# The first layer's modulation: half of its vector moved from TensorE to products on GpSimd and row sums on ScalarE

## The reference, cut to what matters

```python
mod = jax.nn.silu(c) @ ada_w[l] + ada_b[l]        # ada_w: (2, 1024, 6144); the same with c_ctx
sh1, sc1, g1, sh2, sc2, g2 = jnp.split(mod, 6, axis=-1)
h = _rms_norm(x, norm1_g) * (1 + sc1) + sh1
proj = h @ w_in                                   # then three head groups on slices of proj
mix = jnp.concatenate([o_a, o_b, o_c], axis=-1) @ w_out
x = x + g1 * mix
h2 = _rms_norm(x, norm2_g) * (1 + sc2) + sh2
x = x + g2 * (jnp.square(jax.nn.relu(h2 @ w_ff1)) @ w_ff2)
```

## Time and profile before

| | us |
|---|---|
| median of 3 runs (lowest, highest) | 1972.09 (1968.6, 1974.33) |
| the profiled execution | 1966.85 |
| its span | 1965.1 |
| TensorE busy in the span | 1847.0 (94%) |
| VectorE busy | 1092.5 (56%) |
| ScalarE busy | 681.3 (35%) |
| GpSimd busy | 468.1 (24%) |

### The profile page before, as it was taken

How to read it: one execution, slowest core, us unless ns; L and a number is a source line. 1 busy time by engine, 2 the same in 40 slices (tenths; PEclk the granted TensorE clock), 3 DMA queues, 4 the chain that set the end, 5 groups by cost and what they waited for, 6 DMA issues and landing times. The chain is left out here.

```text
span 1965.1 us, 32477 instructions
## 1 busy us (share of the span) xinstructions
PE 1847.0 (94%) x13959; PEld 1750.8 (89%) x13959; DVE 1092.5 (56%) x1629; ACT 681.3 (35%) x1045; POOL 468.1 (24%) x334
## 2 busy tenths in 40 slices
PE   5999989887999999999999999988799999999996
PEld 3899967676999999999999997667799999999996
DVE  3687765665645676766655576557564232323332
ACT  2464346422342131312336534652223223131231
POOL 4000010344342140503530001014524204031244
PEclk9999999998999999999999999989899999999998
DMA  8643120101133444444231212010121212221211
GB/s 350 246 173 90 65 71 2 39 2 60 65 140 108 151 147 157 146 146 144 69 138 66 74 69 71 1 39 2 49 76 66 85 65 74 78 86 65 86 44 54
DMA packets 50527, 179.70 MB, mean 91 GB/s; under 512 B 21616, under 2 KB 23408, under 8 KB 34768
## 3 DMA queue, kind: packets, MB, share of 16 engines
q1 hardware_dynamic: 48848, 176.14, 25.7%
q10 hardware_dynamic: 1536, 1.48, 0.2%
HBM read 168.84 MB, written 8.68 MB: 90 GB/s over the span
## 5 line engine op out<-in xcount | busy, mean ns | idle before, releaser
L1491 PE MATMUL PS<-HH,HI 128*128 128x322 f32 (+1 forms) x1792 | 417.4, 314 | 4.7 <-DVE HL L980 4.7
L1491 PE MATMUL PS<-HL,HI 128*128 128x322 f32 (+1 forms) x1792 | 414.3, 312 | 0.0
L1491 PE MATMUL PS<-HH,LO 128*128 128x322 f32 (+1 forms) x1792 | 413.5, 312 | 0.0
L641 ACT CAST HI<-RAW 128x2048 fp32r<-128x2048 f32 x96 | 182.9, 1905 | 469.3 <-PE PS L1491 442.5
L1491 PEld LDWEIGHTS PS<-HH,HI 128*128 128x128 f32 x1792 | 303.1, 190 | 5.2 <-issue 5.1
L1491 PEld LDWEIGHTS PS<-HH,LO 128*128 128x128 f32 x1792 | 305.3, 191 | 0.0
L1491 PEld LDWEIGHTS PS<-HL,HI 128*128 128x128 f32 x1792 | 304.3, 191 | 0.0
L1491 PE MATMUL PS<-FH,HI 128*128 128x320 f32 x1280 | 293.1, 310 | 1.4 <-DVE FLO L1382 1.4
L1491 PE MATMUL PS<-FH,LO 128*128 128x320 f32 x1280 | 291.4, 309 | 0.0
L973 DVE TENSOR_TENSOR LO<-RAW,HI 128x2048 fp32r<-128x2048 f32 x96 | 232.6, 2423 | 99.5 <-ACT HI L641 99.5
L1491 PE MATMUL PS<-FL,HI 128*128 128x320 f32 x1152 | 262.5, 309 | 0.0
(11 more groups left out here) (282 smaller groups left out, 2254.1 us busy)
## 6 DMA issues: line engine op xcount, KB each, us to landing
RAW<-ws SPq DMA_DIRECT2D x96, 1024.0 KB, 4.9
WM<-adt SPq DMA_DIRECT2D x48, 512.0 KB, 3.6
ADA<-ada SPq DMA_DIRECT2D x16, 1024.0 KB, 7.4
WMX<-adt SPq DMA_DIRECT2D x16, 512.0 KB, 3.7
X<-xT SPq DMA_DIRECT2D x1, 2560.0 KB, 15.7
X<-xT SPq DMA_DIRECT2D x2, 1280.0 KB, 5.9
xs<-X SPq DMA_DIRECT2D x1, 2560.0 KB, 7.9
X<-xs SPq DMA_DIRECT2D x2, 1280.0 KB, 5.5
```

What stands on the lines that cost most here:

```text
L641: nc.scalar.copy(HI[g % 2][:, :], RAW[g % 2][:, :]).then_inc(hi_ready, 1)
L1491: last = pe.matmul(bank(2 * u + a)[:, 0:e], w[:, cols], m[:, a, 0:e], start=(k == 0 and f), stop=(k == KT - 1 and e_))
```

## The change

Columns 16 to 31 leave TensorE. For each of the 16 columns GpSimd multiplies a 128x1024 tile of transposed weights (`WMY`, two buffers, loaded by SyncE) with each condition into `PP[0]` and `PP[1]`, and ScalarE sums `PP[g]` along its row with an accumulating Identity, in place, into `MODN`. GpSimd makes a product of column `n` only when ScalarE has summed the same condition's product of column `n - 1`. ScalarE's sums stand in slots 2 to 12, behind `tile_out`, as many columns a slot as `MOD_IN` says. TensorE's pieces and turns, VectorE's copies and the 1 MB loads go. The new loads stand in SyncE's program behind the slot's `WMX` loads and wait for GpSimd's products. VectorE's slot 13 and ScalarE's slot 21 wait for all products, slot 18 for all sums. The weights are laid out a second way on the host (`adt` gets 16 more tiles).

```diff
+        WMY = [place(f"WMY{i}", [P, D], F32, r_t + i * 4096) for i in range(2)]
+        PP = [place(f"PP{g}", [P, D], F32, r_o + g * 4096) for g in range(2)]
@@ SyncE
-                    def ada_load(j):
-                        sp.dma_start(ADA[3 * (j % 2)][:, :, :], t["ada"][0, 8 + j]).then_inc(ada_in[j % 2], 16)
+                    def gate_load(n):
+                        sp.dma_start(WMY[n % 2][:, :], t["adt"][MF + MT + n]).then_inc(gw_in[n % 2], 16)
@@ SyncE, slot s, behind the WMX loads of the slot
-                        if l == 0 and 1 <= s <= 6:
-                            sp.wait_ge(S["ada_mm"], o["ada_mm"] + s)
-                            ada_load(s + 1)
+                        if l == 0 and s in MOD_IN:
+                            first = sum(MOD_IN[x] for x in MOD_IN if x < s)
+                            for n in range(first + 2, min(first + MOD_IN[s] + 2, MF)):
+                                sp.wait_ge(gprod, 2 * n - 2)
+                                gate_load(n)
@@ GpSimd, ahead of the clearing of LW
+                    def gate_products(n):
+                        if n == 0:
+                            pool.wait_ge(silu_c, 2)
+                        pool.wait_ge(gw_in[n % 2], 16 * (n // 2 + 1))
+                        for g in range(2):
+                            if n:
+                                pool.wait_ge(gsum, 2 * n - 1 + g)
+                            nc.gpsimd.tensor_tensor(PP[g][:, :], WMY[n % 2][:, :], CBX[:, g, :], ALU.mult).then_inc(gprod, 1)
+                    if l == 0:
+                        for n in range(MF):
+                            gate_products(n)
@@ ScalarE, slot j
                         if j == Z0 + 1 and l == 0:
-                            act.wait_ge(S["ada_mm"], 8)
+                            act.wait_ge(gprod, 2 * MF)
                         if j >= 1:
                             tile_out(j - 1)
...
+                        first = sum(MOD_IN[x] for x in MOD_IN if x < j)
+                        for n in range(first, first + MOD_IN.get(j, 0) if l == 0 else first):
+                            for g in range(2):
+                                act.wait_ge(gprod, 2 * n + g + 1)
+                                nc.scalar.activation(PP[g][:, :], PP[g][:, :], ACT.Identity,
+                                                     accum_out=MODN[:, 2 * KT + n, g:g + 1]).then_inc(gsum, 1)
                         if 0 <= j - 3 < 12:
                             conv_silu(j - 3)
@@ ScalarE, slot 18
-                            if l == 0:
-                                act.wait_ge(S["ada_tr"], 8)
@@ VectorE
-                        if l == 0 and 2 <= j <= 9:
-                            ada_row(j - 2)
@@ VectorE, slot 13 and slot 18
+                            dve.wait_ge(gprod, 2 * MF)
-                                dve.wait_ge(S["ada_tr"], 8)
+                                dve.wait_ge(gsum, 2 * MF)
                                 dve.wait_ge(modn, MF)
-                                link(ada_bias(2 * KT, 4 * KT, VEC[:, 2 * KT:4 * KT]))
-                                link(row_bias(4 * KT, 6 * KT, VEC))
+                                link(row_bias(2 * KT, 6 * KT, VEC))
@@ TensorE, slot j
-                        if l == 0 and 1 <= j <= 8:
-                            ada(j - 1)
-                        if l == 0 and 2 <= j <= 9:
-                            adt(j - 2)
```

More of the change, by code:

```diff
@@ L124 @@
     xtr=4, xa=16, xb=16, xo=4, xhi=8, xlo=8, f1_re=32, f1_hi=32, f1_sq=32, f1_lo=32,
-    ada_mm=8, ada_ev=8, ada_tr=8, mod_done=1, moda_done=2)
+    mod_done=1, moda_done=2)
 def build(nc, t):
@@ L324, in build @@
         pro_mm, pro_ev, pro_tr, pro_mod = sem("pro_mm"), sem("pro_ev"), sem("pro_tr"), sem("pro_mod")
-        ada_in = [sem("ada_in0"), sem("ada_in1")]
+        gw_in, gprod, gsum = [sem("gw_in0"), sem("gw_in1")], sem("gprod"), sem("gsum")
         y_fg, y_out = sem("y_fg"), sem("y_out")
@@ L418, in _ @@
                     if l == 0:
-                        ada_load(0)
-                        ada_load(1)
+                        gate_load(0)
+                        gate_load(1)
                     for s in range(PT_ - 2):
@@ L1036, in _ @@
                     o, g0 = base(l), l * CHUNKS
[L1038 to L1044, removed]
                     def taps(i):
@@ L1521, in _ @@
                     o, g0, t0 = base(l), l * CHUNKS, l * TILES
[L1523 to L1533, removed]
                     pe.wait_ge(S["h_sl"], 2 * l + 1)
@@ L1977, in lay_out @@
         "ada": c(tiles(a["ada_w"][0:1], AC).reshape(1, 6 * D // AC, P, KT, AC)),
-        "adt": c(np.concatenate([a["ada_w"][0].T.reshape(MT, P, D)[MT - MF:], a["ada_w"][1].T.reshape(MT, P, D)])),
+        "adt": c(np.concatenate([a["ada_w"][0].T.reshape(MT, P, D)[MT - MF:], a["ada_w"][1].T.reshape(MT, P, D),
+                                 a["ada_w"][0].T.reshape(MT, P, D)[MF:2 * MF]])),
         "crow": c(np.stack([a["c"][0], a["c_ctx"]]).reshape(2, D)),
```

## The result

The changed kernel takes 2029.15 us (median of 4 runs, 2027.02 to 2030.88) against 1971.9 us before (median of 4). The ratio is 1.0291 (95% interval 1.0272 to 1.031): 57 us slower. The forecast was 2024 us, the range 2003 to 2046. The two profiled executions, 1966.85 and 2030.88 us, lie 64.0 us apart, 6.8 more than the medians. What follows on slots is read from these two, so its sums are of 64 and not of 57; where the 6.8 lie isn't shown.

The account below looks back on a forecast made before the run. TensorE was taken to set the pace, VectorE close behind. Products' 61.5 us on VectorE less 3.3 of copies and some 6 of cover gave 52: 1965.1 to 2017 us, 2024 against the median, range 2003 to 2046.

Parts of the forecast that it names:

- TensorE's saving is worth nothing: Slots 2 to 12: the 13.8 us that TensorE saves fall into its waits and win nothing.
- The prices: Slots with modulation: a GpSimd product of 128x1024 takes 2.35 us, a ScalarE row sum 1.25 us.
- Exclusion: Slots 2 to 11: GpSimd products and VectorE operations with two SBUF inputs take turns; 2005 to 2043 us, chance 0.76.
- 2.05 us per product, less 6 of cover: Slots 2 to 11: 30 products each add 2.05 us to VectorE, less 3.3 for copies, some 6 cover: 52.
- the walk: VectorE's odd and even slots followed step by step: 17.5 us becomes 29.2, +11.7 per pair, 52 over slots 2-11.
- The lead: TensorE cannot keep its 9.0 us lead over VectorE at slot 12, so tile 13 is late by about 52 us.
- Its signs: In the profile after: GpSimd busy 75 to 110 us, sums up to 3.5, TensorE's eviction waits 40 to 65, clock unchanged.
- The gain arrives: Slots with modulation: products find VectorE idle or are not held, TensorE's 13.8 us come off; 1958 to 1969 us, chance 0.03.
- nothing moves: Slots with modulation: VectorE goes on at its pace as the true second bound; 1966 to 1978 us, chance 0.02.
- GpSimd gives way: VectorE is always served first, GpSimd is late, splits and taps slip; 10 to 28 us, 1982 to 2000, chance 0.07.
- The queues lock together: ScalarE waits for products, VectorE for ScalarE, TensorE for copies; 3 to 6 us more per pair, 2043 to 2060, chance 0.12.

Follow-up runs that it names:

- when everything went: Changed kernel without products, row sums and their loads, TensorE's gate pieces also gone: 1963.9 us, 3.3 under before, ratio 0.9979.
- The same queue with and without reads: Changed kernel with third weight buffer and loads ahead of modulation loads: 2024.44 us, 57.2 over before; with memsets replacing its products: 1973.81 us, 6.4 over.
- the run with early loads: Changed kernel with a third buffer for the product's weights, their loads ahead of the modulation loads in SyncE's queue: 2024.44 us, ratio 1.0291.

## Why the prediction was right

**TensorE's saving is worth nothing.** Right: by the rows it is 13.8 us, and only 3.3 came off the time when everything went. VectorE's near bound was read rightly from its slots.

**The prices.** Right. The products of the changed kernel (min, median, max in ns):

```profile
L543 POOL TENSOR_TENSOR PP<-WMY,CBX x32: 2339/2446/4438, 67.1 to 221.7; 128x1024 f32<-128x1024 f32 x32
L747 ACT ACTIVATE PP<-PP x32: 1039/1057/1066, 70.5 to 229.9; 128x1024 f32<-128x1024 f32 x32
L747 ACT ACTIVATION_READ_ACCUMULATOR PP<-PP x32: 183/186/188, 71.5 to 230.8; 128x1 f32 x32
```

2339 ns where nothing holds them (2.35 said), and 1057 + 186 ns for a sum (1.06 + 0.19).

**Exclusion.** Shown: products alone on the kernel before cost 58.7 us, their cycle with a sum is 3.34 us (3.31 said), and a sum is back at 1221 ns beside memsets. The same queue with and without reads is 57.2 against 6.4, of which the shorter memsets can explain 23 at most. That only VectorE operations with two SBUF inputs are held was wrong: in the groups above a TENSOR_SCALAR of 40 columns with one tile as input took 2428 ns, 0.18 before. In the changed kernel such small operations lost some 5.5 us.

**2.05 us per product, less 6 of cover.** The term was a little large by itself: 1.83 at full width with 32 in a row, 1.7 with 8, and at half width 0.73 for 0.97. The sum, 52, came out at 62.3 in VectorE's slots: the products hold VectorE directly for only 37.6 us, 1.25 each, but its waits for ScalarE add 26.5, of which the walk had counted the split's in the even slots, and slot 8's as nearly nothing. Two terms of the walk were clearly too small. Slot 5 was taken as any odd slot (4 us), but its exponentials stand behind the sums too: VectorE waits 8.8 us there, and the slot grew by 8.5, from 9.6 to 18.1. And slot 8 grew by 11.3, from 13.1 to 24.4, where the walk's even slot had 7.7 and 1 or 2 on top. By pairs, from slots 2 and 3 to slots 10 and 11, VectorE lost 8.3, 18.3, 5.9, 15.2 and 14.7 us, where the walk had 7.7, 11.7, 11.7, 10.8 and 9.9. So the sum is better than its parts: the pair of slots 6 and 7 was priced at twice what it cost, and its split was the one of five that waited for nothing. And that 2024 us lies 5 us from the median is in part luck: VectorE's slots lost 10 us more than the 52, but of the 64 us between the profiled executions only 57 are between the medians.

**The lead.** Right in what it gives: tile 13 starts 7.9 us after slot 12 (9.0 before), so it is late by about as much as VectorE. The timeline of TensorE:

```profile
233.97 0.56 PE L1501 MATMUL PS<-HH,HI 128*128 128x322 f32 x2
```

Why it can't use its lead was rightly put down to ScalarE's roots and key copies, which stand behind the sums (41 us of waits).

**Its signs.** TensorE's waits were forecast as 40 to 65 us behind evictions. The amount is right (54), the place is not: evictions end 4.2 us, ScalarE 41. The clock was forecast as before, and fell to 0.79 in the mean. It made TensorE's work longer, by an estimated 21 us (133.7 for 124.3 less the 11.7 of gate work). But no row shows that this decided anything: in slots 2 to 12 VectorE waits 1.1 us for a tile of TensorE (1.3 before) and ScalarE's high halves 2.5 us (7.7 before). The other signs came: GpSimd busy 87.5 us, sums up to 3.38 us, slot 12 at 226, and the same time from slot 13 to the end, so the new wait there costs nothing, as said.

**The rivals.** "The gain arrives", "nothing moves" and "GpSimd gives way" fall with the 3.32 us sums. "The queues lock together" exists, as the 14 to 25 us of the late loads, but it runs beside exclusion, not on top of it. That the two cover each other is shown in VectorE's groups (37.6 us held and 32.7 of waits for ScalarE with late loads, 56.4 and 10.9 with early ones). Why they do so nearly in full stays argued: with late loads VectorE idles while GpSimd is at work, with early ones it is held instead.

## What to carry to other kernels

Before work goes to an idle engine, count the instructions of the near-critical engine that it can hold, and price it by its own duration, not by the idle engine's room: here 32 products of 2.35 us took 58 us from a kernel that could win 3. Read the second bound first: when it follows the first within a few microseconds per slot, relieving the first is worth only that. And when two stalls cover the same time, removing one shows nothing; run the square of both, with stand-ins whose length is read from the trace.

## What was not expected of the hardware

A VectorE operation of 40 columns can wait through more than one product. VectorE's timeline in the run with early loads:

```profile
138.02 2.37 DVE L1126 SCALAR_TENSOR_TENSOR SMALL<-SMALL 128x40 f32<-128x40 f32 x1
140.42 4.72 DVE L1128 SCALAR_TENSOR_TENSOR SMALL<-SMALL 128x40 f32<-128x40 f32 x1
```

The second takes 4.72 us for what took 0.20 before. GpSimd's timeline at that place:

```profile
137.89 4.84 POOL L541 TENSOR_TENSOR PP<-WMY,CBX 128x1024 f32<-128x1024 f32 x2
...
142.70 2.38 POOL L541 TENSOR_TENSOR PP<-WMY,CBX 128x1024 f32<-128x1024 f32 x1
```

The first row is two products, the second of them from 140.29; the third begins as it ends, and VectorE, waiting since 140.42, is done at 145.14, behind that one too. The turns seen in the earlier trace rows aren't strict. Groups of GpSimd memsets, 1.6 to 2.0 us long, leave VectorE's sums at 1221 ns.
